# Expert gates of a two-block model: some of the one-hot rows are made on GpSimd

## Chip, cores and metric

The kernel runs on one core of one Trainium2 chip. The metric is the device time of one execution in microseconds (us), the median of several runs. The engines are named as the profile names them: PE (TensorE matmul), PEld (its weight loads), DVE (VectorE), ACT (ScalarE), POOL (GpSimd) and SP (SyncE); ACTq and SPq are the queues of ACT and SP, with their DMA issues.

## What is computed

The program is one transformer block (windowed attention, a state-space scan, a gated merge and a retrieval of single-neuron experts) followed by a second block of two layers, over 256 tokens of width 2048 in float32. Only the expert retrieval of the first block matters here. Each token picks 8 x 16 = 128 of 16384 experts by two key numbers between 0 and 127 and a weight:

```python
idx = jnp.take_along_axis(cand_idx, pos, axis=-1)     # i1 * 128 + i2
gate = jax.nn.softmax(top_s, axis=-1)
...
act = jnp.einsum('tkd,td->tk', u_sel, hb)             # rows of expert_down
w = gb * jax.nn.gelu(act, approximate=False)
return jnp.einsum('tk,tkd->td', w, v_sel)             # rows of expert_up
```

The kernel does not gather. It multiplies the tokens with all of `expert_down` and `expert_up`, and between the two it needs for every token a 128 x 128 table of gates: zero, but for the weights of the chosen experts.

## The kernel before

The first half of `expert_down` ("down0", 64 tiles on PE) leaves the activations of 64 rows of experts in `ab` (128 partitions x 64 x 256 tokens). Then comes the gate stage, and then the first half of `expert_up` ("up0", PE line 2174), which reads `ab` times the gates.

The gate stage takes the tokens in 32 groups of eight. `kt` holds the two key numbers and `gp` the weights, with the 128 chosen experts of a token on the partitions and the 256 tokens along the free dimension. For a group n:

- DVE (`onehots`, line 1520) compares the first key with `iota` (0 to 127) for eight tokens in one instruction and writes eight one-hot rows `oh1[:, n % 2]` (128 x 1024), then does so with the second key for `oh2[:, n % 2]`. Both inputs lie in SBUF. Before `oh2` it waits until PE has finished group n - 2 (`gate_mm`).
- ACT (`gates_weigh`, line 713) multiplies each of the eight rows of `oh1` with the token's weights and writes `gw[:, n % 2]`: eight instructions of 128 x 128.
- PE (`gates_pe`, line 2157) multiplies `oh2` with `gw` for each token: eight float32 products, each shown as two matmul records, into two of the eight PSUM banks.
- DVE (`scale`, line 1526) multiplies the lower half of the table, from PSUM, into `ab` (512 columns).
- ACT (`gates_stage`, line 726) copies the upper half from PSUM to `stage[:, n % 2]`, and `gates_store` (line 734) issues a DMA of it to `g_out` in HBM; the second half of the experts reads it much later.

`oh1`, `oh2`, `gw` and `stage` have two buffers, the PSUM results four. The order on each queue is written out by hand. DVE runs `onehots(n)`, then `scale(n - 2)`. ACT runs `gates_weigh(n)`, `gates_stage(n - 2)`, `gates_store(n - 3)`. Groups 4 to 31 are a loop of seven turns of four groups; the groups before are written out. `gates_stage(m)` waits until the store of group m - 2 has landed, since it writes the same `stage` buffer; and the store of m - 1 is issued behind `gates_stage(m)`. POOL has nothing in this stage; it makes low parts of weights (`lo_split`, line 388) and small tables (lines 1046 to 1049) in earlier stages, and in later ones `h2_lo` (line 1081).

The lines that issue one group's work, and the waits ahead of them:

```python
for ready in ("oh2_ready", "gw_ready"):
    pe.wait_ge(S(ready), g(1))
...
if 2 <= n < 31 or i is not None:
    act.wait_ge(S(f"g_stored{n % 2}"), at(16 * (n // 2), i, 8 * s))
```

Of the kernel before, what the change touches and what calls it, by code (L numbers as in the profile page):

```python
# [19 lines left out]
ALU = mybir.AluOpType  # L20
# [11 lines left out]
TOPK = 16  # L32
PH = 8
SELECT = 13
MLAH = 8
ALPHA = float(4 ** 0.25)
TURN = 6.283185
# [146 lines left out]
def build(nc, stream, vecs, consts, x_in, ctx_in, ssm_b, ssm_c, subkeys, out):  # L184
    es = ExitStack()
    with es:
# [287 lines left out]
        def _(act):  # L474
# [221 lines left out]
                    down_act(t, i * 4 + j)  # L696

            act.wait_ge(S("sel_shifted"), 1)
            act.activation(sv[:], sv[:], ACT.Exp).then_inc(S("sel_exp"), 1)
            with act.Fori(0, 16 - SELECT, 1) as i:  # L700
                for j in range(4):
                    t = Tile("down0", j, i, 4, skip=4 * SELECT)
                    hi_split(act, t.next())
                    down_act(t, i * 4 + (j + 4 * SELECT))
            act.sem_inc(S("acts_done"), 1)

            def gates_weigh(n, i=None, s=0):

                g = of_group(n, i, s)
                act.wait_ge(S("oh1_ready"), g(1))  # L710
                act.wait_ge(S("gate_mm"), g(1))
                for t in range(8):
                    m = act.activation(gw[:, n % 2, t], oh1[:, n % 2, t], ACT.Copy, scale=gp[:, tokens(n, i, s, t, 1)])  # L713
                m.then_inc(S("gw_ready"), 1)

# [19 lines left out]
                              staged(n).rearrange("p c t r -> p c (t r)").unsqueeze(2))\  # L735
                    .then_inc(S(f"g_stored{n % 2}"), 16)

            act.wait_ge(S("kt_ready"), 1)
            for n in range(4):
                gates_weigh(n)  # L740
            gates_stage(0)
# [148 lines left out]
            def act_out(name, layer, n):  # L890

                act.wait_ge(S("mixed"), 1 + layer)
                if layer:
                    act.copy(h2_hi[:, 12:16, T:N2], q1[:, 12:16]).then_inc(S("mx_hi"), 1)
                else:
                    act.copy(h2_hi[:, 12:16], mx[:, 12:16]).then_inc(S("mx_hi"), 1)
                if layer == 0:
                    act.wait_ge(S("x_moved"), 16)
                    act.dma_start(XX[:, :, 0:T], x_save).then_inc(S("x_moved"), 16)
                    act.dma_start(XX[:, :, T:N2], ctx_in).then_inc(S("x_moved"), 16)  # L900
                def scaled(q):
                    if layer == 0:
                        x = XX[:, 4 * q:4 * q + 4, 0:n]
                        m = act.activation(x, x, ACT.Copy, scale=ALPHA)
                    else:
                        for k in range(4 * q, 4 * q + 4):
                            x = XX[:, k, 0:n]
                            m = act.activation(x, x, ACT.Identity, bias=V("lnb", k), scale=V("lng", k))
                    m.then_inc(S("xx_scaled"), 1)

                def square(i):
                    act.wait_ge(S("ln_cent"), 16 * layer + i + 1)
                    if i >= 4:
                        act.wait_ge(S("ln_sqadd"), 15 * layer + max(1, i - 4))
                    act.activation(lns[:, i % 4, 0:n], XX[:, i, 0:n], ACT.Square).then_inc(S("ln_sq"), 1)

                def mean(r, count):
                    act.wait_ge(S("ln_sum"), 3 * layer + r + 1)
                    act.activation(lnm[:, 0:n], bank(6, n), ACT.Copy, scale=1.0 / count).then_inc(S("ln_mean"), 1)

                for k in range(16):
                    hi_split(act, Tile(name, k).next())
                    if k < 2:
                        if layer == 0:
                            act.wait_ge(S("x_moved"), 48)
                        scaled(2 * k)
                        scaled(2 * k + 1)
                    if k == 5:
                        mean(0, 4 * P)
                    for i in CENTER.get(k - 1, ()):  # L930
                        square(i)
                    if k == 14:
                        sqrt_table()
                square(15)
                mean(1, D)
                act.wait_ge(S("ln_acc"), 4 + 4 * layer)
                act.activation(lnr[:, 0, 0:n], lnr[:, 0, 0:n], ACT.Sqrt, bias=V("eps")).then_inc(S("ln_root"), 1)

            act_out("aout", 0, N2)

# [87 lines left out]
        def _(pool):  # L1028
# [43 lines left out]
            with pool.Fori(0, 4, 1) as i:  # L1072
                for j in range(4):
                    lo_split(pool, Tile("wq", j, i, 4).next(), 0)


            for p in range(8):
                c = slice(2 * p, 2 * p + 2)
# [25 lines left out]
        def _(dve):  # L1104
# [109 lines left out]
            for j in range(8):  # L1214
                t = Tile("u", j)
                lo_split(dve, t.next(), 1)
                dve.wait_ge(mm_done, t.done())
                dve.tensor_scalar(qku[:, 20 + j], bank(t.bank(), T), 1.0, None, ALU.mult)\
                    .then_inc(acc_free[t.bank()], 1)
                if j == 0:  # L1220
                    decay()
                if j == 1:
                    dve.wait_ge(S("ht_ready"), 4)
                    L(dve.memset(csp[:], 0.0))
                    dve.wait_ge(S("cs_ready"), 1)
                    dve.tensor_copy(csp[:, :, 0:2], cs[:]).then_inc(S("csp_ready"), 1)
                if j == 3:
                    gains()
                if j == 4:
                    dve.wait_ge(S("h_dve"), 4)  # L1230
                    phases_dve(0)
            for b in range(4):
                dve.wait_ge(acc_free[b], 2)
            dve.sem_inc(S("u_ready"), 1)
            for j in range(4):
                lo_split(dve, Tile("v", j).next(), 1)
                if j == 2:
# [239 lines left out]

            def weights_found():

                dve.wait_ge(S("sel_exp"), 1)  # L1480
                L(dve.tensor_reduce(mt[:, 0:16], sv[:].rearrange("p a h k -> p (a h) k"), AX, ALU.add))
                L(dve.reciprocal(mt[:, 16:32], mt[:, 0:16]))
                for tt in range(2):
                    L(dve.tensor_tensor(ix[:, tt, 2].rearrange("p (h k) -> p h k", k=TOPK), sv[:, tt],
                                        mt[:, 16 + 8 * tt:24 + 8 * tt].unsqueeze(2).to_broadcast([P, PH, TOPK]),
                                        ALU.mult))
                dve.sem_inc(S("ix_ready"), 1)

            dve.wait_ge(lo_done[0], N0["down0"] + 1)
            for n in range(64):  # L1490
# [13 lines left out]
                dve.tensor_copy(kt[:, n], bank(4 + n, T))  # L1504
            dve.wait_ge(S("ix_turned"), 3)
            L(dve.tensor_copy(gp[:], bank(6, T)))
            dve.sem_inc(S("kt_ready"), 1)
            dve.wait_ge(mm_done, G0["up0"])

            def onehots(n, i=None, s=0):  # L1510

                g = of_group(n, i, s)
                if i is not None or n >= 2:
                    dve.wait_ge(S("gw_ready"), g(-1))
                for o, f, ready in ((oh1, 0, S("oh1_ready")), (oh2, 1, S("oh2_ready"))):
                    if f:
                        dve.wait_ge(S("gate_mm"), g(1))
                    key = kt[:, f, tokens(n, i, s)].unsqueeze(2).to_broadcast([P, 8, P])
                    io = C("iota").unsqueeze(1).to_broadcast([P, 8, P])
                    dve.tensor_tensor(o[:, n % 2], key, io, ALU.is_equal).then_inc(ready, 1)  # L1520

            def scale(n, i=None, s=0):

# [5 lines left out]
            onehots(0)  # L1529
            onehots(1)  # L1530
            onehots(2)
            dve.wait_ge(S("acts_done"), 1)
            dve.wait_ge(acc_free[(A0["up0"] - 1) % 4], (A0["up0"] - 1) // 4 + 2)
            scale(0)
            onehots(3)
# [209 lines left out]
            def dve_out(name, layer, n):  # L1745
# [28 lines left out]
                for k in range(16):  # L1774
# [28 lines left out]
                dve.wait_ge(S("ln_sum"), 3 * layer + 3)  # L1803
                dve.scalar_tensor_tensor(lnr[:, 0, 0:n], bank(7, n), 1.0 / D, lnr[:, 0, 0:n], ALU.mult, ALU.subtract)\
                    .then_inc(S("ln_acc"), 1)
                dve.wait_ge(S("ln_root"), 1 + layer)
                L(dve.reciprocal(lnr[:, 1, 0:n], lnr[:, 0, 0:n]))

                def shift(k):
# [125 lines left out]
        def _(pe):  # L1935
# [27 lines left out]
            for j in range(4):  # L1963
                t = Tile("v", j)
                wait_weights(pe, t)
                for tt in range(2):
                    o = Tile("v", tt)
                    if j == 0:
                        pe.wait_ge(acc_free[o.bank()], o.bank_free())
                    for c in range(4):  # L1970
                        for n, (x, w) in enumerate(((h_hi, w_hi), (h_hi, w_lo), (h_lo, w_hi))):
                            m = pe.matmul(bank(o.bank()), x_tok(x, 4 * j + c, tt), w[:, t.par, 4 * c:4 * c + 4],
                                          start=(j + c + n == 0), stop=(j == 3 and c == 3 and n == 2))
                m.then_inc(mm_done, 1)
                if j == 1:
                    pe.wait_ge(S("u_ready"), 1)
                    bu(0)

            def mod_tile(t, q):
# [27 lines left out]
                        if n == 3:  # L2007
                            m.then_inc(S("out_done"), 1)

            pe.wait_ge(S("csp_ready"), 1)  # L2010
            q = 0
            bu(1)
            for u in range(UNITS):
# [122 lines left out]
                    dense(pe, Tile("down0", j, i, 4), xh1, xl1)  # L2136
            for j in range(60, 64):
                if j == 63:
                    pe.wait_ge(S("ix_ready"), 1)
                    for n in range(3):  # L2140
                        for tt in range(2):
                            m = pe.transpose(bank(4 + n, P, tt * P), ix[:, tt, n], C("ident"))
                        m.then_inc(S("ix_turned"), 1)
                dense(pe, Tile("down0", j), xh1, xl1)
            pe.wait_ge(S("kt_ready"), 1)
            pe.sem_inc(S("gate_mm"), 2)

            def gates_pe(n, i=None, s=0):

                g = of_group(n, i, s)  # L2150
                if i is not None or n >= 4:
                    pe.wait_ge(S("gates_in"), g(-3))
                    pe.wait_ge(S("g_staged"), g(-3))
                for ready in ("oh2_ready", "gw_ready"):
                    pe.wait_ge(S(ready), g(1))
                for t in range(8):
                    m = pe.matmul(gate_banks(n)[:, t], oh2[:, n % 2, t], gw[:, n % 2, t], start=True, stop=True)  # L2157
# [413 lines left out]
```

## Time and profile before

| | us |
|---|---|
| median of three runs | 4132.77 |
| the three runs | 4132.93, 4121.27, 4132.77 |
| span of the profiled execution, first to last instruction | 4120.0 |
| gate stage, first one-hot to the first matmul of up0 | 1482.9 to 1580.5 |
| PE busy, of the span | 3900.4 |
| POOL busy, of the span | 843.8 |

The profiled execution's own time is not listed apart from its span. The run nearest to it, 4121.27, lies 1.3 us above the span, the median 12.8 us.

A row of a timeline is: start, duration, engine, line, operation, tiles out<-in, shapes, how many instructions are merged in it, and in brackets the idle time of the engine ahead of it with what ended that. Starts of successive instructions on one engine tell its pace better than durations, since the end of one overlaps the start of the next.

### The profile page before, as it was taken

What the parts mean: (1) busy time and instruction counts of PE and PEld (TensorE: products, weight loads), DVE (VectorE), ACT (ScalarE), POOL (GpSimd) and SP (SyncE); (2) the same over time, 40 slices, a digit from 0 to 9 for tenths busy, and PEclk for the clock granted to TensorE, in tenths of its full rate; (3) what the DMA queues carried; (4) which work ended last, traced back from release to release, by engine and by line L of the source; (5) the groups of instructions that cost most, each with busy time, mean ns of one, the idle gap of its engine ahead of it and who ended that gap; (6) DMA issues with size and microseconds to landing.
All of it is one profiled execution on the core that took longest, in us unless ns stands there. A gap on an engine that the chain in (4) does not pass through costs nothing.

```text
span 4120.0 us, 72977 instructions
## 1 busy us (share of the span) xinstructions
PE 3900.4 (95%) x30180; PEld 3573.1 (87%) x30180; DVE 2403.9 (58%) x3403; ACT 1655.9 (40%) x2312; POOL 843.8 (20%) x611
## 2 busy tenths in 40 slices
PE   7999998899999988999999999999999899979997
PEld 6777677899999978999999999999999557758887
DVE  5999966543777676555555555533232334657656
ACT  3223335544355575333444334422222123243674
POOL 3877852234300000000000000000000002133223
PEclk9999999999999999999999999999999889989999
DMA  5887763355455544555555555422222103213323
GB/s 211 306 302 289 296 260 126 109 183 181 169 194 194 190 129 159 193 193 214 212 213 212 200 193 193 174 90 95 96 98 92 41 31 113 92 62 133 123 103 133
DMA packets 132295, 679.34 MB, mean 165 GB/s; under 512 B 43665, under 2 KB 49937, under 8 KB 52369
## 3 DMA queue, kind: packets, MB, share of 16 engines
q1 hardware_dynamic: 89952, 641.77, 42.9%
q10 hardware_dynamic: 42160, 35.01, 2.6%
q8 instruction: 131, 2.15, 0.2%
q14 instruction: 52, 0.42, 0.0%
HBM read 664.15 MB, written 12.58 MB: 164 GB/s over the span
## 4 chain that ended last, share of the span: by engine, by line
PE 78%; DVE 13%; ACT 4%; issue 3%; POOL 1%; DMA 1%; ACTq 0%; DVEq 0%; POOLq 0%
PE banks L410 49%; PE banks L2174 17%; PE banks L2294 1%; DVE w_lo L388 1%; PE banks L2085 1%; DVE pq L1283 1%; DVE banks L1273 1%; PE banks L2349 1%; PE banks L2243 1%; PE banks L2242 1%; ACT w_hi L380 1%; DVE rq L1319 1%; DVE banks L1260 1%; ACT gw L713 1%; PE banks L2415 1%
## 5 line engine op out<-in xcount | busy, mean ns | idle before, releaser
L410 PE MATMUL banks<-h_hi,w_hi 128*128 128x256 f32 (+1 forms) x6176 | 1653.3, 288 | 83.1 <-DVE w_lo L388 29.6
L410 PE MATMUL banks<-h_hi,w_lo 128*128 128x256 f32 (+1 forms) x6176 | 1632.3, 285 | 0.0
L410 PE MATMUL banks<-h_lo,w_hi 128*128 128x256 f32 (+1 forms) x6176 | 1631.8, 285 | 0.0
L380 ACT CAST w_hi<-ring 128x1024 fp32r<-128x1024 f32 x986 | 984.9, 1048 | 1011.9 <-PE banks L410 431.4
L388 DVE TENSOR_TENSOR w_lo<-ring,w_hi 128x1024 fp32r<-128x1024 f32 x798 | 993.0, 1276 | 600.4 <-ACT w_hi L380 596.8
L410 PEld LDWEIGHTS banks<-h_hi,w_hi 128*128 128x128 f32 x6176 | 1115.1, 190 | 150.1 <-issue 110.3
L410 PEld LDWEIGHTS banks<-h_hi,w_lo 128*128 128x128 f32 x6176 | 1114.2, 190 | 15.4 <-issue 0.5
L410 PEld LDWEIGHTS banks<-h_lo,w_hi 128*128 128x128 f32 x6176 | 1113.3, 190 | 14.8
L388 POOL TENSOR_TENSOR w_lo<-ring,w_hi 128x1024 fp32r<-128x1024 f32 x188 | 480.9, 2558 | 1667.3 <-ACT w_hi L380 1665.8
L2174 PE MATMUL banks<-wp_hi,w_hi 128*128 128x256 f32 x2048 | 567.9, 277 | 5.2 <-DVE wp_lo L1553 5.1
L2174 PE MATMUL banks<-wp_hi,w_lo 128*128 128x256 f32 x2048 | 567.5, 277 | 0.0
L2174 PE MATMUL banks<-wp_lo,w_hi 128*128 128x256 f32 x2048 | 567.5, 277 | 0.0
L2174 PEld LDWEIGHTS banks<-wp_hi,w_hi 128*128 128x128 f32 x2048 | 386.0, 188 | 5.7 <-DVE ab L1592 3.6
L2174 PEld LDWEIGHTS banks<-wp_hi,w_lo 128*128 128x128 f32 x2048 | 386.0, 188 | 0.0
L2174 PEld LDWEIGHTS banks<-wp_lo,w_hi 128*128 128x128 f32 x2048 | 385.9, 188 | 0.0
L1081 POOL TENSOR_TENSOR h_lo<-xc,h_hi 128x512 fp32r<-128x512 f32 x8 | 10.3, 1288 | 1448.5 <-ACT h_hi L782 1448.5
L1551 DVE TENSOR_SCALAR wp_hi<-ab 128x256 fp32r (+1 forms) x128 | 37.6, 294 | 261.7 <-PE banks L2174 261.5
L685 ACT ACTIVATE ab<-banks 128x256 f32 (+1 forms) x128 | 49.1, 384 | 335.9 <-PE banks L410 335.7
L1046 POOL TENSOR_TENSOR cst<-tab 128x256 f32<-128x256 f32 x128 | 102.6, 801 | 72.8 <-DVE pq L1283 67.2
L1049 POOL TENSOR_TENSOR rot<-cst 128x256 f32<-128x256 f32 x128 | 97.6, 762 | 10.0
L1047 POOL TENSOR_TENSOR cst<-tab 128x256 f32<-128x256 f32 x128 | 96.3, 752 | 0.0
L2157 PE MATMUL banks<-gw,oh 128*128 128x128 f32 x512 | 67.2, 288 | 28.8 <-ACT gw L713 28.8
(377 smaller groups left out, 4280.7 us busy)
## 6 DMA issues: line engine op xcount, KB each, us to landing
ring<-in_stream_dram SPq DMA_DIRECT2D x555, 1024.0 KB, 4.8
spare<-in_stream_dram SPq DMA_DIRECT2D x30, 1024.0 KB, 6.2
cst<-in_stream_dram SPq DMA_DIRECT2D x23, 1024.0 KB, 5.9
g_in<-g_out ACTq DMA_DIRECT2D x8, 1024.0 KB, 6.6
g_out<-stage ACTq DMA_DIRECT2D x31, 256.0 KB, 2.6
X<-in_x_in_dram SPq DMA_DIRECT2D x2, 1024.0 KB, 7.1
b_st<-in_ssm_b_dram ACTq DMA_DIRECT2D x8, 256.0 KB, 8.1
c_st<-in_ssm_c_dram ACTq DMA_DIRECT2D x8, 256.0 KB, 5.6
```

Source lines behind the costliest of these rows:

```text
L380: act.copy(w_hi[:, t.par, s], weights(t.slot)[:, s]).then_inc(hi_done, 1)
L388: eng.tensor_tensor(w_lo[:, t.par, s], weights(t.slot)[:, s], w_hi[:, t.par, s].bitcast(F32), ALU.subtract).then_inc(lo_done[h], 1)
L410: m = pe.matmul(bank(b, e - a, a), w[:, t.par, k], x(k)[:, a:e], start=first and a == 0, stop=last and e == n, skip_group_check=e - a < n)
L685: act.activation(ab[:, row], bank(t.bank(), T), ACT.Gelu).then_inc(acc_free[t.bank()], 1)
L713: m = act.activation(gw[:, n % 2, t], oh1[:, n % 2, t], ACT.Copy, scale=gp[:, tokens(n, i, s, t, 1)])
L1046: pool.tensor_tensor(rt[:, 0], A_(p0), B_(p1), ALU.mult)
L1047: pool.tensor_tensor(rt[:, 1], A_(p2), B_(p3), ALU.mult).then_inc(S("rt_ready"), 1)
L1049: pool.tensor_tensor(rot[:, u % 3, f], rt[:, 0], rt[:, 1], op).then_inc(S("rot_ready"), 1)
L1260: dve.tensor_tensor(crossed, src, r[:, 1:2].to_broadcast([P, 2, T]), ALU.mult).then_inc(S("bu_free"), 1)
L1273: m = dve.tensor_tensor_scan(scanned[:, z], dec, crossed[:, 1 - z], 0.0, ALU.mult, ALU.add)
L2157: m = pe.matmul(gate_banks(n)[:, t], oh2[:, n % 2, t], gw[:, n % 2, t], start=True, stop=True)
L2174: m = pe.matmul(bank(k // 2, T, k % 2 * T), w[:, t.par, k], x[:, j % 2], start=(first and j == 0 and n == 0 and k % 2 == 0), stop=False, s ...
```

## The change

Two constants, `FUSED = 3` and `POOLED = 6`, split the rows of each group. POOL makes rows 0 to 2 of `gw` in one instruction each, comparing `iota` with the token's first key and multiplying with the token's weight, and rows 6 and 7 of `oh2`, a compare each: five `tensor_scalar` instructions of 128 x 128 per group, 160 in all. DVE makes rows 3 to 7 of `oh1` (640 columns) and rows 0 to 5 of `oh2` (768 columns). ACT weighs rows 3 to 7. PE waits for POOL's rows too. One semaphore, `oh2_pool`, is new, and others are merged: `sel_exp` and `acts_done` become `sel_acts`, `ix_ready` and `kt_ready` become `keys_ready`, `csp_ready` and `u_ready` become `mix_in`, and `ln_root` joins `root`.

```diff
+FUSED, POOLED = 3, 6
...
-            act.sem_inc(S("acts_done"), 1)
+            act.sem_inc(S("sel_acts"), 1)
...
-                for t in range(8):
+                for t in range(FUSED, 8):
                     m = act.activation(gw[:, n % 2, t], oh1[:, n % 2, t], ACT.Copy, scale=gp[:, tokens(n, i, s, t, 1)])
                 m.then_inc(S("gw_ready"), 1)
...
-            act.wait_ge(S("kt_ready"), 1)
+            act.wait_ge(S("keys_ready"), 2)
...
+            pool.wait_ge(S("keys_ready"), 2)
+            pool.wait_ge(mm_done, G0["up0"])
+            for n in range(32):
+                pool.wait_ge(S("gate_mm"), n + 1)
+                for t in range(FUSED):
+                    e = 8 * n + t
+                    pool.tensor_scalar(gw[:, n % 2, t], C("iota"), kt[:, 0, e:e + 1], gp[:, e:e + 1],
+                                       ALU.is_equal, ALU.mult)
+                for t in range(POOLED, 8):
+                    e = 8 * n + t
+                    m = pool.tensor_scalar(oh2[:, n % 2, t], C("iota"), kt[:, 1, e:e + 1], None, ALU.is_equal)
+                m.then_inc(S("oh2_pool"), 1)
...
-                    dve.tensor_tensor(o[:, n % 2], key, io, ALU.is_equal).then_inc(ready, 1)
+                m = 8 - FUSED
+                key = kt[:, 0, tokens(n, i, s, FUSED, m)].unsqueeze(2).to_broadcast([P, m, P])
+                io = C("iota").unsqueeze(1).to_broadcast([P, m, P])
+                dve.tensor_tensor(oh1[:, n % 2, FUSED:], key, io, ALU.is_equal).then_inc(S("oh1_ready"), 1)
+                dve.wait_ge(S("gate_mm"), g(1))
+                key = kt[:, 1, tokens(n, i, s, 0, POOLED)].unsqueeze(2).to_broadcast([P, POOLED, P])
+                io = C("iota").unsqueeze(1).to_broadcast([P, POOLED, P])
+                dve.tensor_tensor(oh2[:, n % 2, 0:POOLED], key, io, ALU.is_equal).then_inc(S("oh2_ready"), 1)
...
-                for ready in ("oh2_ready", "gw_ready"):
+                for ready in ("oh2_ready", "oh2_pool", "gw_ready"):
                     pe.wait_ge(S(ready), g(1))
...
-                    pe.wait_ge(S("u_ready"), 1)
+                    pe.wait_ge(S("mix_in"), 2)
```

## Rows read from the trace of the kernel before

**Rows 1.** The page's first part: busy us (share of the span), instructions.
```profile
PE 3900.4 (95%) x30180; PEld 3573.1 (87%) x30180; DVE 2403.9 (58%) x3403; ACT 1655.9 (40%) x2312; POOL 843.8 (20%) x611
```

**Rows 2.** Busy time by stretch: us, then PE, PEld, DVE, ACT, POOL; clock.
```profile
1494.00:1576.00 82.00, 58.00 (x461) 53.27 (x459) 81.82 (x86) 81.50 (x259) 0.00 (x0) 1.00 0.34 90
```

**Rows 3.** Waits of the gate stage, longest first: total us, times, longest.
```profile
PE banks L2157 <- ACT gw L713: 28.8, 30, 3.9
```

**Rows 4.** Timeline of DVE in the loop.
```profile
1555.10 0.67 DVE L1526 TENSOR_TENSOR ab<-ab,banks 128x512 f32 x1
1555.70 2.35 DVE L1520 TENSOR_TENSOR oh<-kt,cst 128x1024 f32<-128x1024 f32 x2
1557.97 0.67 DVE L1526 TENSOR_TENSOR ab<-ab,banks 128x512 f32 x1
```

**Rows 5.** Timeline of ACT in the loop.
```profile
1559.91 2.16 ACT L713 ACTIVATE gw<-oh,gp 128x128 f32<-128x128 f32 x7
1561.79 0.38 ACTq L734 DMA_DIRECT2D g_out<-stage  x1
1561.97 0.39 ACT L713 ACTIVATE gw<-oh,gp 128x128 f32<-128x128 f32 x1
1562.27 0.57 ACT L726 ACTIVATE stage<-banks 128x512 f32<-128x512 f32 x1
1562.78 2.15 ACT L713 ACTIVATE gw<-oh,gp 128x128 f32<-128x128 f32 x7
```

**Rows 6.** Timeline of PE at the stage's start, in the loop and at the end.
```profile
1486.82 8.53 PE L2157 MATMUL banks<-gw,oh 128*128 128x128 f32 x48 [3.94 <-ACT gw L713]
...
1559.63 2.02 PE L2157 MATMUL banks<-gw,oh 128*128 128x128 f32 x16 [0.82 <-ACT gw L713]
...
1576.85 2.02 PE L2157 MATMUL banks<-gw,oh 128*128 128x128 f32 x16 [0.84 <-ACT gw L713]
```

**Rows 7.** Timeline of DVE and ACT at the stage's start.
```profile
1482.92 5.77 DVE L1520 TENSOR_TENSOR oh<-kt,cst 128x1024 f32<-128x1024 f32 x5 [1.30 <-PE banks L410]
1484.23 4.79 ACT L713 ACTIVATE gw<-oh,gp 128x128 f32<-128x128 f32 x16 [0.83 <-DVE oh L1520]
```

**Rows 8.** Timeline of ACT at the end of the stage.
```profile
1576.10 0.38 ACTq L734 DMA_DIRECT2D g_out<-stage  x1
...
1578.77 0.60 ACT L726 ACTIVATE stage<-banks 128x512 f32<-128x512 f32 x1 [1.59 <-DMA g_out<-stage]
1578.79 0.39 ACTq L734 DMA_DIRECT2D g_out<-stage  x1
```

**Rows 9.** The tile `stage`: issue of its stores to their landing.
```profile
DMA to landing us min/median/max: 2.6/2.6/3.1
```

**Rows 10.** Timeline of POOL and DVE, 301 to 308, in the mix stage.
```profile
301.06 0.62 POOL L1046 TENSOR_TENSOR cst<-tab 128x256 f32<-128x256 f32 x1
301.64 0.62 POOL L1047 TENSOR_TENSOR cst<-tab 128x256 f32<-128x256 f32 x1
...
302.97 0.41 DVE L1265 TENSOR_TENSOR banks<-td,banks 128x256 f32<-128x256 f32 x1
303.15 2.40 POOL L388 TENSOR_TENSOR w_lo<-ring,w_hi 128x1024 fp32r<-128x1024 f32 x1
303.30 0.42 DVE L1266 TENSOR_TENSOR banks<-td,banks 128x256 f32<-128x256 f32 x1
303.63 3.00 DVE L388 TENSOR_TENSOR w_lo<-ring,w_hi 128x1024 fp32r<-128x1024 f32 x1
...
305.50 1.61 POOL L1046 TENSOR_TENSOR cst<-tab 128x256 f32<-128x256 f32 x1
```

**Rows 11.** Timeline of DVE, 319 to 323, while POOL runs lines 1046 to 1049.
```profile
319.73 0.91 DVE L1185 TENSOR_TENSOR ph<-ph 128x256 f32<-128x256 f32 x1
...
322.19 0.71 DVE L1188 TENSOR_SCALAR ph<-ph 128x256 f32<-128x256 f32 x1
```

**Rows 12.** Timeline of POOL and DVE, 3613 to 3622, in the last layer.
```profile
3613.55 7.27 POOL L1092 TENSOR_TENSOR h_lo<-hmr,h_hi 128x512 fp32r<-128x512 f32 x2 [23.42 <-ACT h_hi L954]
...
3617.18 0.68 DVE L1811 TENSOR_TENSOR XX<-XX,lnm 128x512 f32<-128x512 f32 x1
3617.78 0.68 DVE L1826 TENSOR_TENSOR XX<-XX,lnr 128x512 f32<-128x512 f32 x1
```

**Rows 13.** Groups of POOL instructions by line and shape: count, busy, mean ns, idle.
```profile
L1081 POOL TENSOR_TENSOR h_lo<-xc,h_hi 128x512 fp32r<-128x512 f32 x8 | 10.3, 1288 | 1448.5 <-ACT h_hi L782 1448.5
...
L2562 POOL MEMSET const-float32-1.0<- 128x1 f32 x1 | 0.1, 98 | 0.0
```

More of the change, by code:

```diff
@@ L698, in _ @@
             act.wait_ge(S("sel_shifted"), 1)
-            act.activation(sv[:], sv[:], ACT.Exp).then_inc(S("sel_exp"), 1)
+            act.activation(sv[:], sv[:], ACT.Exp).then_inc(S("sel_acts"), 1)
             with act.Fori(0, 16 - SELECT, 1) as i:
@@ L936, in act_out @@
                 act.wait_ge(S("ln_acc"), 4 + 4 * layer)
-                act.activation(lnr[:, 0, 0:n], lnr[:, 0, 0:n], ACT.Sqrt, bias=V("eps")).then_inc(S("ln_root"), 1)
+                act.activation(lnr[:, 0, 0:n], lnr[:, 0, 0:n], ACT.Sqrt, bias=V("eps")).then_inc(S("root"), 1)
             act_out("aout", 0, N2)
@@ L1225, in _ @@
                     dve.wait_ge(S("cs_ready"), 1)
-                    dve.tensor_copy(csp[:, :, 0:2], cs[:]).then_inc(S("csp_ready"), 1)
+                    dve.tensor_copy(csp[:, :, 0:2], cs[:]).then_inc(S("mix_in"), 1)
                 if j == 3:
@@ L1233, in _ @@
                 dve.wait_ge(acc_free[b], 2)
-            dve.sem_inc(S("u_ready"), 1)
+            dve.sem_inc(S("mix_in"), 1)
             for j in range(4):
@@ L1478, in weights_found @@
             def weights_found():
-                dve.wait_ge(S("sel_exp"), 1)
+                dve.wait_ge(S("sel_acts"), 1)
                 L(dve.tensor_reduce(mt[:, 0:16], sv[:].rearrange("p a h k -> p (a h) k"), AX, ALU.add))
@@ L1486, in weights_found @@
                                         ALU.mult))
-                dve.sem_inc(S("ix_ready"), 1)
+                dve.sem_inc(S("keys_ready"), 1)
             dve.wait_ge(lo_done[0], N0["down0"] + 1)
@@ L1506, in _ @@
             L(dve.tensor_copy(gp[:], bank(6, T)))
-            dve.sem_inc(S("kt_ready"), 1)
+            dve.sem_inc(S("keys_ready"), 1)
             dve.wait_ge(mm_done, G0["up0"])
@@ L1514, in onehots @@
                     dve.wait_ge(S("gw_ready"), g(-1))
[L1515 to L1519, printed above, removed]
-                    dve.tensor_tensor(o[:, n % 2], key, io, ALU.is_equal).then_inc(ready, 1)
+                m = 8 - FUSED
[6 more added lines that the diff above has]
+                dve.tensor_tensor(oh2[:, n % 2, 0:POOLED], key, io, ALU.is_equal).then_inc(S("oh2_ready"), 1)
             def scale(n, i=None, s=0):
@@ L1531, in _ @@
             onehots(2)
-            dve.wait_ge(S("acts_done"), 1)
+            dve.wait_ge(S("sel_acts"), 2)
             dve.wait_ge(acc_free[(A0["up0"] - 1) % 4], (A0["up0"] - 1) // 4 + 2)
@@ L1805, in dve_out @@
                     .then_inc(S("ln_acc"), 1)
-                dve.wait_ge(S("ln_root"), 1 + layer)
+                dve.wait_ge(S("root"), 3 + layer)
                 L(dve.reciprocal(lnr[:, 1, 0:n], lnr[:, 0, 0:n]))
@@ L2008, in ssm_out @@
                             m.then_inc(S("out_done"), 1)
-            pe.wait_ge(S("csp_ready"), 1)
+            pe.wait_ge(S("mix_in"), 2)
             q = 0
@@ L2138, in _ @@
                 if j == 63:
-                    pe.wait_ge(S("ix_ready"), 1)
+                    pe.wait_ge(S("keys_ready"), 1)
                     for n in range(3):
@@ L2144, in _ @@
                 dense(pe, Tile("down0", j), xh1, xl1)
-            pe.wait_ge(S("kt_ready"), 1)
+            pe.wait_ge(S("keys_ready"), 2)
             pe.sem_inc(S("gate_mm"), 2)
```

## The prediction

> **What bounds the kernel now.** The page's busy shares come first: PE is busy 95% of the span and POOL 20% [rows 1], so nearly everything is PE's. The gate stage is the exception, and the change touches no other stage. I read it next by stretch: from 1494 to 1576 PE is busy 58.0 of 82 us at granted clock 1.00 (the upper level, 2.4 GHz), while DVE is busy 81.8, ACT 81.5 and POOL not at all [rows 2]. The list of waits says whom PE waits for: ACT's weighted rows, 28.8 us in 30 waits [rows 3]. A wait names only what came last, so I timed both full engines by their starts.
>
> DVE goes from one `scale` to the next in 1557.97 - 1555.10 = 2.87 us: 0.60 for the scale and 2.27 for the two one-hot instructions, 1.135 each [rows 4]. ACT needs eight rows at (1561.97 - 1559.91) / 7 = 0.294 and 0.51 for the copy to `stage`: 2.86 [rows 5]. Both set the pace, within 0.01 us; PE's own work is 2.02 [rows 6]. Relieving one alone would buy nothing. The change relieves both, so the question is what comes next.
>
> Two things are nearly late already. **The stores.** The store of one group waits behind the copy of the next, and that copy waits until the store before has landed. At the end of the stage, where ACT has no rows left to weigh, this shows: the store issued at 1576.10 ends the wait of the copy at 1578.77, and the next store goes out at 1578.79 [rows 8]. That loop takes 2.69 us, and its landing is steady, 2.6 at least and 2.6 in the median [rows 9]. It is hidden now under 2.86 of ACT work, by only 0.17. **The way into SBUF that DVE and POOL share.** A DVE one-hot reads two SBUF operands, as `lo_split` does. When POOL held SBUF operands from 303.15 to 305.55, a DVE `lo_split` begun at 303.63 took 3.00 instead of 1.135 and ended at 306.63, 1.08 behind POOL's end; the POOL instruction begun at 305.50 in turn took 1.61 instead of 0.62 [rows 10]. In that time DVE instructions with an operand in PSUM kept their 0.42. In the last layer two POOL instructions ended 7.27 us after 3613.55, though 1.29 each is their undisturbed time [rows 12, 13]: DVE's run of instructions on SBUF operands went on until 3618.46, and 2.36 us behind its end both were done. So the two engines take turns, instruction by instruction, and the whole instruction counts.
>
> **The change part by part.**
> DVE: the 512-column instruction's pace is 0.60 [rows 4, 12] and the 1024-column one's 1.135, so a column costs 0.535 / 512 = 1.045 ns and an instruction 0.065 us. 640 columns take 0.734 and 768 take 0.867, 1.60 together; with the scale DVE needs 2.20 per group, 0.67 less.
> ACT: three rows less, 5 x 0.294 + 0.51 = 1.98, 0.88 less.
> PE: the same 2.02, and one more wait.
> POOL: 5 new instructions of 128 columns per group, 160 in all. No row shows a `tensor_scalar` on POOL, so its price c is bounded. From below, an instruction that reads nothing and writes one column takes 0.098 [rows 13]. From above, a two-operand one of 256 columns, twice the columns and one stream more, paces at 301.64 - 301.06 = 0.58 [rows 10]. Between them: half of 0.58 is 0.29. How long such an instruction keeps DVE out is read where the two alternate: three DVE steps take 322.19 - 319.73 = 2.46 [rows 11], 0.82 each, of which DVE's own pace is 0.33 (303.30 - 302.97, rows 10); 0.49 remains for POOL's 256 columns, 0.245 for 128. I take c = 0.27, the middle: one stream less than the measured instruction, but two per-partition scalars to fetch, which nothing here shows.
>
> The sum: DVE's one-hots and POOL's rows take turns, the scale (PSUM) can lie beside POOL. The period is P = 1.60 + 5c = 1.60 + 1.35 = 2.95, above DVE's 2.20, ACT's 1.98, PE's 2.02 and the stores' 2.69. DVE does not keep POOL out for good as in rows 12, because its `oh2` waits for PE, which now waits for POOL.
>
> From period to time: the stage starts at 1482.92 [rows 7]. The first group now reaches PE at 1486.82, behind one one-hot and eight weighed rows, the last group at 1576.85 [rows 6]. After the change the first group's share of the port is done P later, PE follows 0.14 behind (as it now follows ACT's eighth row, which ends at 1484.23 + 7 x 0.294 + 0.39 = 1486.68), and the last group comes 31 periods on: the end moves by 1482.92 + 0.14 + 32P - 1576.85 = 32P - 93.8. With P = 2.95 that is +0.6 us. Break-even is 2.93; now the stage runs 31 intervals at 2.90, and gains at its start what the loop loses.
>
> The Trainium skill, page "GPSIMD Engine Reference", section "Performance versus the Vector engine", gives about 1.03 cycles an element at 1.2 GHz for POOL bodies of at most two operations, an estimate of 0.11 us for 128 columns where the rows' two-operand pace gives 0.29. By the page P would be 1.60 + 0.55 = 2.15, under the stores' loop. No run here shows a one-operand instruction on POOL; this is the first rival.
>
> **The added waits.** PE's wait for POOL holds the eight products of the group, and with them DVE's scale, ACT's copy and POOL's own rows two groups on. Behind POOL's waits stands nothing else until line 1081, for which POOL idles 1448 us [rows 13], so POOL's lateness costs this stage alone.
>
> **At nothing:** the shared semaphores. Both increments of `mix_in` and of `sel_acts` come in program order from one engine, and `keys_ready` and `root` are waited for at the count that their last increment gives; nothing becomes ready later. The copy of `cs` that now also stands ahead of `bu(0)` runs in the second of eight u tiles on the same DVE queue. Without that order its cost would be one small copy.
>
> **The rivals.**
> *The port is not the limit.* POOL's instructions are short (c below 0.22), or let DVE through. For it: one tensor operand instead of two. Against: DVE's 3.00 [rows 10]. Then the stores' loop comes last: P = 2.69, end moves by 32 x 2.69 - 93.8 = -7.7, 4125. Still within what counts as the same.
> *POOL is dear: slower.* Place: POOL's five instructions between PE's group n - 2 and group n. If c is over 0.344, P is over 3.32 and the loss over 12.4 us. For it: two operations and two scalar operands per instruction, a shape that no row shows, and the bound of 0.58 is not excluded. With c = 0.45, P = 3.85 and the loss is 29 us, 4162; at 0.58, P = 4.50, the loss is 50. Against: columns, not instructions, set POOL's price (2.40 for 1024, 0.58 to 0.62 for 256, rows 10).
> *Faster.* The stores land sooner than 2.45 us and POOL's rows are nearly free of the port: P down to DVE's 2.20 and -23 us, 4109. Against: the least landing is 2.6 [rows 9], and the copy at 1578.77 shows that loop with ACT idle.
>
> The skill's page "SBUF — State Buffer", section "A bandwidth-pool intuition that's wrong (but worth ruling out)", has the blocked engine start some 115 ns behind the other's end. With four turnovers a group that would make P 2.95 + 0.46 = 3.41 and the loss 15 us. Here DVE ended 1.08 behind POOL, less than its own 1.135 [rows 10], so the trace shows no such gap; such a gap has 0.03 of the slower rival's 0.28.
>
> **How the numbers follow.** 0.3% of 4132.77, about what a measurement of this kernel can tell from no change, is 12.4 us. The sum is made on the profiled execution of span 4120.0 and added to the median, which is 12.8 higher. The forecast, P between 2.83 (c = 0.245) and 3.32, has 0.47: from -3 to +12, 4129 to 4145, with 4134 at P = 2.95. The port not the limit: 0.17. POOL dear: 0.28. Faster: 0.08. So same 0.64, slower 0.28, faster 0.08. The range reaches down past 4125 by the spread of the runs, to 4117, and up to c = 0.45, 4162; what is dearer and the faster rival are left out, about 2 in 10.
>
> **What would show it.** Right: POOL's starts in the loop some 0.3 apart where DVE stands still, DVE one-hots of 0.73 and 0.87 stretched by whole POOL instructions, `scale` unstretched at 0.67, PE waiting for POOL rather than ACT, ACT idle about 0.9 a group, PE groups 2.8 to 3.3 apart. The store rival: copies to `stage` waiting for the DMA in the loop, 2.69 to 2.75 apart. Wrong: `tensor_scalar` over 0.35 undisturbed, or one-hots unstretched beside POOL.

## The result, and the profile after

The changed kernel takes 4184.35 us, the median of four runs (4168.32 to 4206.72), against 4131.08 for the kernel before (four runs, 4121.27 to 4132.93). The ratio is 1.0135, with a 95% interval of 1.01 to 1.0171: slower, by about 53 us, and outside the range of the prediction.

The profiled execution took 4206.72, the longest of the four. The gate stage, from the first one-hot to the first matmul of up0, now lasts from 1481.2 to 1636.5, 155.3 us instead of 97.6. That is +57.7, and it covers the whole difference of the medians. Nearly all of the other 27 of the profiled execution's +84.8 us of span lies in up0 and down1 and is not the change's (the last section shows why). The stage's end, the first matmul of up0:

```profile
1636.49 0.36 PE L2190 MATMUL banks<-wp_hi,w_hi 128*128 128x256 f32 x1 [1.66 <-DVE wp_lo L1569]
```

The page's first part, to set against [rows 1]:

```profile
PE 3954.8 (94%) x30180; PEld 3620.5 (86%) x30180; DVE 2387.7 (57%) x3403; ACT 1632.9 (39%) x2216; POOL 992.3 (24%) x771
```

The kernel looks almost the same by it; POOL has 160 more instructions and 148.5 us more of busy time. The busy time by stretch of the gate stage, in the columns of [rows 2], says which engine is full:

```profile
1500.00:1550.00 50.00, 28.99 (x172) 26.59 (x171) 25.75 (x33) 23.82 (x66) 49.94 (x55) 0.81 0.22 58
1550.00:1600.00 50.00, 29.80 (x172) 27.37 (x170) 25.92 (x33) 23.81 (x66) 49.94 (x55) 0.80 0.20 53
```

DVE and ACT, full in [rows 2], are half idle, and POOL, idle before, is busy 49.94 of 50 us. PE's granted clock was 1.00 in this stage; now it is 0.80, a mix of the two levels. The waits between 1481 and 1637 (total us, times, longest) agree:

```profile
POOL gw L1084 <- PE banks L411: 352.0, 1, 352.0
ACT gw L714 <- PE banks L2173: 72.0, 25, 6.6
DVE oh L1536 <- PE banks L2173: 71.9, 25, 6.4
...
POOL gw L1084 <- PE banks L2173: 0.5, 1, 0.5
```

The first is POOL's wait for the stage to begin. Inside the stage POOL waits 0.5 us in all, while everyone else waits for PE. PE's own waits are mostly named "issue", by which the profile shows no releaser; what PE lacks is POOL's rows, as POOL alone is never idle. A stage with one engine that is never idle has the period of that engine. So the next view is POOL's and DVE's timeline, first POOL's rows and then DVE's:

```profile
1543.52 3.94 POOL L1084 TENSOR_SCALAR gw<-cst,kt,gp 128x128 f32<-128x128 f32 x3
1547.44 1.74 POOL L1088 TENSOR_SCALAR oh<-cst,kt 128x128 f32<-128x128 f32 x2
1549.17 2.34 POOL L1084 TENSOR_SCALAR gw<-cst,kt,gp 128x128 f32<-128x128 f32 x3
1551.49 1.18 POOL L1088 TENSOR_SCALAR oh<-cst,kt 128x128 f32<-128x128 f32 x2
...
1543.37 0.97 DVE L1536 TENSOR_TENSOR oh<-kt,cst 128x768 f32<-128x768 f32 x1 [3.14 <-PE banks L2173]
1544.26 0.67 DVE L1542 TENSOR_TENSOR ab<-ab,banks 128x512 f32 x1
1544.85 0.81 DVE L1532 TENSOR_TENSOR oh<-kt,cst 128x640 f32<-128x640 f32 x1
1545.80 0.99 DVE L1536 TENSOR_TENSOR oh<-kt,cst 128x768 f32<-128x768 f32 x1
1546.72 0.67 DVE L1542 TENSOR_TENSOR ab<-ab,banks 128x512 f32 x1
1547.31 0.81 DVE L1532 TENSOR_TENSOR oh<-kt,cst 128x640 f32<-128x640 f32 x1
1552.37 0.96 DVE L1536 TENSOR_TENSOR oh<-kt,cst 128x768 f32<-128x768 f32 x1 [4.25 <-PE banks L2173]
```

From 1549.17 to 1552.37 DVE makes no one-hot, and POOL's group is undisturbed: 2.34 for three rows of `gw`, 1.18 for two of `oh2`, 0.78 and 0.59 each and 3.51 together. In the group begun at 1543.52, three one-hots of DVE lie beside the rows, and the three rows take 3.94; the two compares begun at 1547.44 meet a one-hot and take 1.74. They lose 0.56, a little less than the 0.68 that the one-hot still had to go (1547.31 + 0.81 = 1548.12). The compares begun at 1551.49 lose nothing, though a one-hot begins at 1552.37, in the middle of the second. So a POOL row waits for the rest of a one-hot that is running when it begins, and not for one that begins later: over the whole stage, the 13 rows that had run for 0.1 us or more when a one-hot began kept their length within 0.01. Where both begin within 0.06, it goes either way. DVE's instructions keep 0.81 and 0.96 to 0.99. The same over the whole stage (durations in ns: least, median, greatest; then first and last start):

```profile
L1088 POOL TENSOR_SCALAR oh<-cst,kt x64: 593/599/1419, 1486.6 to 1630.4; 128x128 f32<-128x128 f32 x64
L1532 DVE TENSOR_TENSOR oh<-kt,cst x32: 810/817/976, 1481.2 to 1623.0; 128x640 f32<-128x640 f32 x32
L1536 DVE TENSOR_TENSOR oh<-kt,cst x32: 951/959/1196, 1481.9 to 1625.2; 128x768 f32<-128x768 f32 x32
```

POOL's 32 groups run from 1481.3 to 1630.4 + 0.6, 4.68 us each: 3.51 of own work and 1.17 of waiting.

### The profile page after: what moved, and what is told of

It reads as the page before. It is cut to its first block, busy times and chain, and to the rows that moved or that the text cites. A ratio compares the mean times of both kernels' runs of the same rounds, so it can differ in the third digit from the quotient of the medians.

```text
span 4204.8 us, 72960 instructions
## 1 busy us (share of the span) xinstructions
PE 3954.8 (94%) x30180; PEld 3620.5 (86%) x30180; DVE 2387.7 (57%) x3403; ACT 1632.9 (39%) x2216; POOL 992.3 (24%) x771
## 4 chain that ended last, share of the span: by engine, by line
PE 79%; DVE 12%; issue 3%; ACT 3%; POOL 1%; DMA 1%; DVEq 0%; ACTq 0%; POOLq 0%
PE banks L411 49%; PE banks L2190 17%; PE banks L2173 2%; PE banks L2310 1%; DVE w_lo L389 1%; PE banks L2101 1%; DVE pq L1297 1%; DVE banks L1287 1%; PE banks L2365 1%; PE banks L2259 1%; PE banks L2258 1%; ACT w_hi L381 1%; DVE rq L1333 1%; DMA ring<-in_stream_dram 1%; DVE banks L1274 1%
## 5 line engine op out<-in xcount | busy, mean ns | idle before, releaser
L1084 POOL TENSOR_SCALAR gw<-cst,kt,gp 128x128 f32<-128x128 f32 x96 | 102.9, 1080 | 352.6 <-PE banks L411 352.0
L2173 PE MATMUL banks<-gw,oh 128*128 128x128 f32 x512 | 90.1, 349 | 63.6 <-issue 51.5
L2173 PEld LDWEIGHTS banks<-gw,oh 128*128 128x128 f32 x512 | 83.2, 254 | 70.4 <-issue 64.5
L1047 POOL TENSOR_TENSOR cst<-tab 128x256 f32<-128x256 f32 x128 | 105.0, 821 | 73.2 <-DVE pq L1297 67.6
```

Of the source, the lines that this page charges most:

```text
L1047: pool.tensor_tensor(rt[:, 0], A_(p0), B_(p1), ALU.mult)
L1084: pool.tensor_scalar(gw[:, n % 2, t], C("iota"), kt[:, 0, e:e + 1], gp[:, e:e + 1], ALU.is_equal, ALU.mult)
```

## The experiments

The theory after this reading: POOL's five instructions are the bound; 3.51 is their own price and 1.17 is time in which DVE's one-hots hold the shared way into SBUF (argued so far; the experiment with PSUM tests it). In every experiment the length of the stage is read from its profile, since runs of one kernel, the one before included, differ by up to 1% among themselves (4112 to 4154 in 19 runs on one chip).

### What POOL's instructions cost by themselves

The kernel before, with seven kinds of POOL instruction, eight times each, in up0, where POOL is idle. `key` and `wgt` are one column each of `kt` and `gp`. The fourth and fifth instructions have 512 columns, the last 256, the others 128:

```diff
+pool.tensor_scalar(gw[:, 1, 0], C("iota"), key, wgt, ALU.is_equal, ALU.mult)
+pool.tensor_scalar(gw[:, 1, 1], C("iota"), key, None, ALU.is_equal)
+pool.tensor_scalar(gw[:, 1, 2], C("iota"), 1.0, None, ALU.mult)
+pool.tensor_scalar(wide, C("iota", 0, 512), key, None, ALU.is_equal)
+pool.tensor_scalar(sf[:, 0:512], C("iota", 0, 512), key, wgt, ALU.is_equal, ALU.mult)
+pool.tensor_tensor(gw[:, 1, 7], C("iota"), C("perm_m"), ALU.mult)
+pool.tensor_tensor(sf[:, 512:768], C("iota", 0, 256), C("perm_m", 0, 256), ALU.mult) ...
```

> The kernel before, with seven kinds of POOL instructions eight times over during up0 (results unused), where DVE leaves POOL the port for about half of the time; the shortest of each kind is its undisturbed price. In the changed kernel 128 columns cost 0.78 us (compare and multiply) and 0.59 (compare). If the price is per column, 512 columns cost about 3.1 and 2.4. If most of it is a fixed cost per instruction, 512 columns cost less than 1.7 and 1.5, and the multiplication by a constant (no scalar to fetch) costs less than 0.45. A two-operand product of 128 columns: 0.3 if proportional to the 0.58 of 256 columns, as the prediction took it; 0.5 or more if a fixed part stands in it too.

POOL's timeline of this kernel (DVE works on its own tiles beside it, so the least of eight is taken for each kind):

```profile
1638.98 2.07 POOL L1088 TENSOR_SCALAR stage<-cst,kt,gp 128x512 f32<-128x512 f32 x1
...
1643.97 0.79 POOL L1084 TENSOR_SCALAR gw<-cst,kt,gp 128x128 f32<-128x128 f32 x1
1644.74 0.60 POOL L1085 TENSOR_SCALAR gw<-cst,kt 128x128 f32<-128x128 f32 x1
...
1655.64 0.53 POOL L1086 TENSOR_SCALAR gw<-cst 128x128 f32<-128x128 f32 x1
1656.15 1.56 POOL L1087 TENSOR_SCALAR gw<-cst,kt 128x512 f32<-128x512 f32 x1
...
1661.79 0.46 POOL L1089 TENSOR_TENSOR gw<-cst 128x128 f32<-128x128 f32 x1
1662.21 0.74 POOL L1090 TENSOR_TENSOR stage<-cst 128x256 f32<-128x256 f32 x1
```

The fused row has 0.79 here and the plain one 0.60, as in the changed kernel, so these are their own prices. A compare of 512 columns takes 1.56: (1.56 - 0.60) / 384 = 2.5 ns a column and about 0.28 to begin with. Compare and multiply take (2.07 - 0.79) / 384 = 3.3 ns a column and 0.36. The two-operand product of 128 columns has 0.46, the multiplication by a constant 0.53. Neither case of the expectation holds as it stands: 512 columns cost less than four times 128, but more than if most of the price were fixed. Per column the instruction with one tensor operand and two scalars is dearer than the one with two tensor operands, and 128 columns of it (0.79) more than 256 of the other (0.74 here, 0.58 to 0.62 in [rows 10]).

### DVE's one-hots cut to one row each

```diff
-m = 8 - FUSED
+m, m2 = (8 - FUSED, POOLED) if i is None and n < 2 else (1, 1)
```

> The changed kernel, but from group 2 on DVE makes one row of each one-hot tile instead of five and six (the other rows keep the keys of groups 0 and 1): DVE's time at the port falls from 1.60 us a group to about 0.4, POOL's five instructions stay. Theory A (POOL's own price 3.51 and its waits for DVE's port time): POOL goes from 4.68 a group to 3.6 to 3.9, one-operand instructions at 0.78 and 0.59 with few stretched ones. Theory B (PE at the lower clock is in the loop): the period stays above 4.5. Theory C (POOL's instructions are slow of themselves inside this stage, the port has no part): stays at 4.68.

From the third group on this kernel leaves out DVE's other rows. The stage took 125.4 us. POOL's timeline in the loop:

```profile
1544.54 1.42 POOL L1088 TENSOR_SCALAR oh<-cst,kt 128x128 f32<-128x128 f32 x2
1545.96 2.34 POOL L1084 TENSOR_SCALAR gw<-cst,kt,gp 128x128 f32<-128x128 f32 x3
1548.29 1.43 POOL L1088 TENSOR_SCALAR oh<-cst,kt 128x128 f32<-128x128 f32 x2
```

Now a group takes 1548.29 - 1544.54 = 3.75. Most of the 1.17 went with DVE's columns, and what DVE kept costs POOL 0.24 a group. The waiting follows DVE's work on SBUF; POOL's own 3.51 stays.

### Other splits between the engines

Three kernels move the split. In the first POOL has no rows of `gw` and the two of `oh2`; in the second one row of `gw` and none of `oh2`; in the third three and none.

```diff
-FUSED, POOLED = 3, 6
+FUSED, POOLED = 0, 6
```

> The changed kernel with FUSED 0: POOL makes rows 6 and 7 of oh2 alone, two instructions of 0.59, DVE eight rows of oh1 and six of oh2, ACT weighs all eight. Theory A: POOL needs 1.18 and at most 1.5 of waits, under ACT's 2.86, so the stage is as before, PE waits for ACT at granted clock 1.00, and the time is within 5 us of before. Rival (any POOL row in the loop costs its wait for DVE in PE's path): period over 3.0, more than 4 us slower.

> The changed kernel with FUSED 1 and POOLED 8: POOL makes one weighted row per group, DVE seven and eight rows, ACT seven. Theory A: POOL 0.78 and at most 1.5 of waits; DVE needs 2.74, ACT 2.57, the stores' loop 2.69, so the period is 2.74 to 2.80 and the time 2 to 5 us less than before. Rival (DVE's port time of 2.1 in 2.7 us leaves POOL no room): period over 2.9, same or slower.

> The changed kernel with FUSED 3 and POOLED 8: POOL makes the three weighted rows alone, 2.34 us undisturbed; DVE makes oh1 of five rows and oh2 of eight (1.87 us at the port), ACT weighs five. Theory A (price, and waits for DVE's one-hots): one wait of about 1.1 behind oh2 and sometimes one behind oh1, so 3.4 to 4.0 a group and the stage 15 to 34 us longer than the 97.6 of before, 0.4% to 0.8% slower. If the dear part of the change were only the number of instructions, the two rows of oh2 would have mattered as much as these three: they cost nothing by themselves (plain2).

| split (rows of `gw`, of `oh2` on POOL) | stage, us | us, median | ratio to before, 95% |
|---|---|---|---|
| before: 0, 0 | 97.6 | | |
| 0, 2 | 97.8 | 4135.19 | 1.0012 (0.9978 to 1.0046) |
| 1, 0 | 95.5 | 4126.67 | 0.998 (0.9953 to 1.0007) |
| 3, 0 | 145.4 | 4187.07 | 1.013 (1.0074 to 1.0186) |
| the change: 3, 2 | 155.3 | 4184.35 | 1.0135 (1.01 to 1.0171) |

As long as POOL's share is small it has time to wait for PE (0.85 a group in the first), and nothing is lost. One row shows the collision at its clearest. POOL, then DVE, in the kernel with one row:

```profile
1542.61 1.85 POOL L1084 TENSOR_SCALAR gw<-cst,kt,gp 128x128 f32<-128x128 f32 x1 [1.18 <-PE banks L2173]
...
1542.66 1.23 DVE L1536 TENSOR_TENSOR oh<-kt,cst 128x1024 f32<-128x1024 f32 x1 [0.20 <-PE banks L2173]
1543.80 0.68 DVE L1542 TENSOR_TENSOR ab<-ab,banks 128x512 f32 x1
```

Both are released by the same end of a PE group. POOL starts 0.05 ahead, and yet DVE goes through in 1.23 and the row of 0.78 needs 1.85: it ends 0.57 behind DVE's one-hot (1544.46 against 1543.89). Where both begin together, the row that POOL has just begun does not keep DVE's one-hot out.

The third split cost more than expected, 47.8 us over the 97.6 of before instead of 15 to 34. Its period is 4.39: POOL's 96 rows are busy for 125.8 us, 3.93 a group, of which 2.34 is their own price and 1.59 waiting; the other 0.46 is idle time:

```profile
L1084 POOL TENSOR_SCALAR gw<-cst,kt,gp 128x128 f32<-128x128 f32 x96 | 125.8, 1321 | 377.7 <-PE banks L411 363.1 <-PE banks L2173 14.6
```

The 14.6 us are waits for PE, which I had not counted; the clock of this stage was 0.78, and whether PE would have been in time at the full clock was not tried apart.

### Two rows, with `scale` between the one-hots

```diff
-FUSED, POOLED = 3, 6
+FUSED, POOLED = 2, 8
...
 dve.tensor_tensor(oh1[:, n % 2, FUSED:], key, io, ALU.is_equal).then_inc(S("oh1_ready"), 1)
+if i is not None:
+    scale(n - 2, i, s)
 dve.wait_ge(S("gate_mm"), g(1))
```

> The changed kernel with FUSED 2 and POOLED 8, and in the loop DVE's scale put between the two one-hots, so that POOL's first instruction reads beside it. POOL needs 1.56 and one wait behind oh2 (1.1), 2.7; DVE 0.87 + 0.60 + 1.135 = 2.60; ACT 2.27; two stage buffers, so the stores' loop of 2.69 to 2.76 stands. Period 2.70 to 2.80, copies to stage that wait for the DMA in the loop, the stage 93 to 95 us against 97.6. Rival (POOL kept out of the port twice per group): period over 2.87, copies do not wait for the DMA.

> The same with four stage buffers (two over the tables rm and rg, which are loaded again after up0 instead of before it): the stores' loop is gone. Period 2.60 to 2.70, set by DVE or POOL, the stage 88 to 92 us, no copy waits for the DMA; the time 6 to 10 us under before, about 0.2%, hardly to be told from no change in the times. If the stores were not the limit, the stage is as long as with two buffers, up to the 2 us at its end.

Both were misses. The stage of the first took 109.2 us, and the rival's condition, a period over 2.87, is what happened (the one run took 4153.0). POOL is again never idle; its timeline merges nineteen rows:

```profile
1529.37 30.84 POOL L1084 TENSOR_SCALAR gw<-cst,kt,gp 128x128 f32<-128x128 f32 x19
```

A row takes 30.84 / 19 = 1.62, a group 3.25, where two rows are worth 1.56. The other order does not spare POOL: DVE's 1.22 and 0.95 then follow each other directly, and POOL waits 1.7 a group. The kernel with four `stage` buffers has 109.5 and a ratio of 1.0039 (1.0014 to 1.0064), so the stores are not the limit here, and its 88 to 92 us were missed for the same reason.

### DVE's second operand in PSUM

This takes the collision away and leaves all the work. `iota` is copied into a PSUM bank ahead of the stage, so that a one-hot reads one operand from SBUF. For the bank, PE's results use two pairs of banks instead of four.

```diff
+dve.tensor_copy(bank(7, P), C("iota"))
...
-io = C("iota").unsqueeze(1).to_broadcast([P, m, P])
+io = bank(7, P).unsqueeze(1).to_broadcast([P, m, P])
...
-b = 2 * (n % 4)
+b = 2 * (n % 2)
```

> The changed kernel, but DVE's one-hot instructions read iota from a PSUM bank instead of SBUF (copied there once ahead of the stage), so that each has one operand in SBUF; for the bank the groups' results use two pairs of banks instead of four. The whole computation stays. Theory (POOL's 1.17 us of waiting a group is the SBUF way it shares with DVE's instructions of two SBUF operands): POOL's rows run at 0.78 and 0.59 throughout, 3.51 a group, the stage takes 115 to 120 us (before 97.6, changed 155.3), the run is near 4150 us. Rival 1 (POOL waits for something else in the loop: a semaphore, the writes of both engines, the order of the queues): 4.5 to 4.7 a group stays and the stage takes 150 to 158. Rival 2 (one SBUF operand halves the contention only): about 4.1 a group, stage 135.

The stage took 115.5 us, as the theory had it. The run took 4176.14 and not 4150; its profile has the slower of PE's two paces (last section) from 1200 to 1300 and from 1660 to 1760, where the kernel before has the faster. POOL and DVE in the loop, and the one-hots of the whole stage:

```profile
1541.57 2.34 POOL L1084 TENSOR_SCALAR gw<-cst,kt,gp 128x128 f32<-128x128 f32 x3
1543.89 1.18 POOL L1088 TENSOR_SCALAR oh<-cst,kt 128x128 f32<-128x128 f32 x2
1545.06 2.33 POOL L1084 TENSOR_SCALAR gw<-cst,kt,gp 128x128 f32<-128x128 f32 x3
...
1543.85 0.95 DVE L1537 TENSOR_TENSOR oh<-kt,banks 128x768 f32<-128x768 f32 x1 [1.20 <-PE banks L2174]
1544.73 0.68 DVE L1543 TENSOR_TENSOR ab<-ab,banks 128x512 f32 x1
1545.32 0.81 DVE L1533 TENSOR_TENSOR oh<-kt,banks 128x640 f32<-128x640 f32 x1
...
L1088 POOL TENSOR_SCALAR oh<-cst,kt x64: 588/592/607, 1505.5 to 1614.1; 128x128 f32<-128x128 f32 x64
L1533 DVE TENSOR_TENSOR oh<-kt,banks x32: 814/815/820, 1503.0 to 1608.0; 128x640 f32<-128x640 f32 x32
```

The one-hots lie right beside POOL's rows, and neither is stretched: the longest plain row has 607 ns where it had 1419. A group takes 1545.06 - 1541.57 = 3.49. All of the 1.17 went with DVE's second operand in SBUF.

The Trainium skill, page "SBUF — State Buffer", section "Who interferes with whom", has DVE contend with a POOL instruction that reads SBUF when both of DVE's inputs lie in SBUF, and not with one. These runs agree: 4.68 with two, 3.49 with one. The section calls the shared pair of ports "an exclusive lock". In the changed kernel's trace that fits POOL, which waits, and not DVE, whose 128x768 one-hot had at most 1196 ns against a median of 959 beside a POOL that is never idle.

Two kernels use this with shares that POOL can carry, and four `stage` buffers so that the stores' 2.69 [rows 8] is no limit:

```diff
-FUSED, POOLED = 3, 6
+FUSED, POOLED = 2, 7
```

> As the kernel with iota in PSUM, with POOL's share cut to what it can do: two rows of gw and one of oh2 a group (2 x 0.78 + 0.59 = 2.15 us), DVE makes 768 and 896 columns, and four stage buffers instead of two, so that the stores' loop of 2.69 does not come last. The whole computation stays. Theory: POOL 2.15, ACT 6 x 0.294 + 0.51 = 2.27, DVE 0.87 + 1.00 + 0.60 = 2.47 a group: the pace is 2.47 to 2.6 and the stage takes 84 to 88 us, 10 to 13 below before, ratio 0.997. Rival (POOL is still kept out by DVE): POOL 2.15 + 1.9 = 4.0 a group, stage about 130, slower than before by 30 us.

> The same with three rows of gw on POOL and none of oh2 (3 x 0.78 = 2.34 us a group); DVE makes 640 and 1024 columns. The whole computation stays. Theory: ACT 1.98, POOL 2.34, DVE 0.73 + 1.135 + 0.60 = 2.47: stage 84 to 88 us, ratio 0.997. With iota in SBUF the same split took 145.4. Rival (POOL is still kept out): about 4.2 a group, stage 135 to 145.

The stages took 88.9 us (two rows of `gw`, one of `oh2`) and 89.2 (three and none), 8.7 and 8.4 less than before and just over the 84 to 88 expected; the split of three and none took 145.4 with `iota` in SBUF. The pace is 1544.66 - 1542.03 = 2.63 by the first one's POOL rows, and PE's rows name what is next, `stage` on ACT, for which PE now waits with two pairs of banks:

```profile
1542.03 1.57 POOL L1088 TENSOR_SCALAR gw<-cst,kt,gp 128x128 f32<-128x128 f32 x2
1543.58 0.60 POOL L1092 TENSOR_SCALAR oh<-cst,kt 128x128 f32<-128x128 f32 x1
1544.66 1.57 POOL L1088 TENSOR_SCALAR gw<-cst,kt,gp 128x128 f32<-128x128 f32 x2 [0.48 <-PE banks L2178]
...
1542.53 2.02 PE L2178 MATMUL banks<-gw,oh 128*128 128x128 f32 x16 [0.61 <-ACT stage L729]
```

In the whole time this can't be seen: the ratios are 0.9998 (0.997 to 1.0026) and 0.9997 (0.9969 to 1.0025), where 8.5 us would be 0.998. No version beat the kernel before beyond its interval.

## Why the prediction was wrong

**The step that failed is POOL's price c, and its bound from above.** The prediction put c at 0.27, between 0.098 and 0.58, the pace of a two-operand instruction of 256 columns, "twice the columns and one stream more". Measured, undisturbed, are 0.78 and 0.59, on the average 3.51 / 5 = 0.70: the one well above what was called the upper bound, the other just at it. The mistake was to order prices by columns and streams of operands. The rows that were read hold no POOL instruction that compares, or that does two operations, or that takes scalars from a tile. At 128 columns the multiplication by a constant has 0.53, the compare with a key from a tile 0.60, the compare and multiply 0.79; what of the last steps is the operation and what the scalar was not tried apart. Even the product of 128 columns has 0.46 and not half of 0.58.

**The port term was too high, and its mechanism half right.** "Take turns, and the whole instruction counts" gave 1.60 a group for DVE's columns. POOL does wait for a one-hot, but only for the rest of one that is running when a POOL row begins; what lies beside a row already begun costs nothing, so 1.17 of the 1.60 remain. DVE in turn hardly waits for POOL, whose rows should have stretched the one-hots. [rows 10] had shown the opposite, a DVE instruction held from 1.135 to 3.00, but beside a POOL instruction of two operands and 1024 columns; it does not carry over to this one. Both signs that the prediction gave for being wrong are there: `tensor_scalar` over 0.35, and one-hots unstretched.

**The formula held.** With P = 4.68, 32P - 93.8 is +56; the stage grew by 57.7. With `iota` in PSUM P = 3.49 gives +17.9, and 115.5 - 97.6 = 17.9 was measured. The two corrections make P = 2.95 + 5 x (0.70 - 0.27) - (1.60 - 1.17) = 4.67; that is no test of its own, since price and waiting were both read from the 4.68, but the 3.51 that it leaves without the port is what the experiment with PSUM found (3.49). So the wrong price was worth about 69 us and the port term -14: the two errors pulled opposite ways.

**What bounds the stage before** was read rightly: with `iota` in PSUM DVE goes from 1543.85 to 1544.73 and to 1545.32, 0.88 and 0.59 where 0.87 and 0.60 were costed, and DVE and ACT were both half idle after. The stage simply had no engine with 3.5 us to spare in a period of 2.9. POOL's share of the rows, 5 of 16, was more than the whole period allows.

**The rivals.** "POOL is dear: slower" is what happened; it named the shape that no row shows, but ended at c = 0.58 and +50 by the same port rule. With c = 0.70 that rule would have given 1.60 + 3.51 = 5.11 and +70; with DVE passing POOL, 57.7 were measured. "The port is not the limit" is right only with one SBUF operand, and there the stores were no limit, since P is 3.49. The estimate by the Trainium skill's page "GPSIMD Engine Reference", section "Performance versus the Vector engine", 0.11 us a row, was a fifth to a seventh of what the runs show.

**The rest.** The merged semaphores cost nothing that shows: the stage began at 1481.2, and at 1482.9 before, while it began anywhere from 1479.3 to 1503.0 in the profiles of the experiments. The low clock is a consequence and no cause: PE's groups take 2.02 or up to 3.75 us, within a period of 4.68, and POOL waited 0.5 us for PE in the whole stage.

## What to carry to other kernels

Before giving work to an idle engine, time one such instruction there; a bound from another form of instruction is none, as a POOL row of 128 columns with scalars from a tile cost more than 256 columns with two tensors. Then compare its share with the period, 5 x 0.70 against 2.90 here. And where DVE and POOL work beside each other, put one of DVE's operands in PSUM: it took away all 1.17 us of POOL's waiting a group, and DVE's instructions kept their length. The price is a bank of PSUM: these kernels gave PE's results two pairs of banks instead of four, and in the last two PE waited for them.

## What was unexpected of the hardware

PE has two paces at granted clock 1.00. Busy time by stretch within up0, of the kernel before and of the changed one:

```profile
1660.00:1760.00 100.00, 100.00 (x885) 100.00 (x884) 56.52 (x73) 36.10 (x36) 0.00 (x0) 1.00 0.55 197
```

```profile
1716.00:1816.00 100.00, 100.00 (x852) 100.00 (x851) 55.46 (x72) 35.90 (x36) 0.00 (x0) 1.00 0.52 187
```

885 matmuls in 100 us are 113 ns each, 852 are 117.4. A stretch without a pause keeps the one pace or the other; over the 3072 matmuls of up0 that is some 13.5 us, and the changed kernel's profiled execution had the slower one in up0 and in down1 (852 from 2100 to 2200). Up0 took 12.8 us longer there than before and down1 13.6, which is nearly all of the 27 us beside the stage's 57.7. It isn't the change: four of the experiments show 851 or 852 between 1200 and 1300, ahead of the stage, where both main profiles have 885 and 884, and the kernel of the prices, whose gate stage is that of before, has 851 from 1750 to 1850. Nor is it the clock of the stage: the split of three and none had 0.78 there, as low as the change, and 884 from 1660 to 1760. Three such stretches, some 40 us, would make up the spread of the runs (4112 to 4154), but only the profiled executions can show it. What chooses the pace was not settled.

Of the clock: in the changed kernel, where PE's groups came 4.68 apart and PE waited between them, the granted clock of the stage was 0.80, between the lower level (1.2 GHz) and the upper (2.4 GHz); with `iota` in PSUM, where they came 3.49 apart, it stayed at 1.00. And POOL's compare costs 2.5 ns a column, its compare and multiply 3.3, with 0.28 and 0.36 to begin with.
